# Two chunk pairs of the second output projection computed by seven block products, and the gate groups of the last decay head split into portions

## The reference

```python
# first block
x = x + y @ w_out            # pooling layer: y is 2048 wide, w_out 2048 x 1024
x = x + y @ w_out            # latent attention, 16 heads of 128: y 2048 wide
x = rmsnorm(x, final_norm)
# second block
h = rms_norm(x, g) @ w_in    # q, k, v, forget gates, z
attn = forgetting_attention(q, k, v, log_f)              # 8 heads of 64, with decay
sgu = zu * (w_s @ layer_norm(zv) + b_s)                  # 8 gate groups of 64
x = x + concat(rms_norm(attn), rms_norm(sgu)) @ w_out
x = x + (silu(gate) * up) @ w_down                       # 2816 wide
out = rms_norm(x, final_norm_g)
```

## Time and profile before

| | |
|---|---|
| median of 3 runs | 1300.34 us (1299.59 to 1300.74) |
| profiled execution | 1299.91 us, span 1298.2 us |
| granted clock of PE | 0.999 over the span |
| PE busy | 1289.8 us of the span, 99% |
| DVE, ACT, POOL busy | 871.9, 596.8, 461.3 us |

### The profile page before, as it was taken

The page is one execution under the profiler, slowest core; times in us unless marked ns, Lnnn a source line. Parts: engine busy times, 40 slices in busy tenths (PEclk is TensorE's granted clock), DMA queues, the critical chain, the costliest instruction groups (busy, mean ns, idle before and its releaser), DMA issues.

```text
span 1298.2 us, 17978 instructions
## 1 busy us (share of the span) xinstructions
PE 1289.8 (99%) x6934; PEld 1095.9 (84%) x6934; DVE 871.9 (67%) x1239; ACT 596.8 (46%) x989; POOL 461.3 (36%) x208
## 2 busy tenths in 40 slices
PE   9999999999999999999999999999999999999998
PEld 7888888898778888888888788898879999998886
DVE  7999726889292366665534574567989999985442
ACT  5223323435343465666733345568464444443223
POOL 2444544445444442443544343323430000015441
PEclk9999999999999999999999999999999999999999
DMA  4333423224722522325143345543323323323331
GB/s 164 98 98 106 123 88 97 77 85 139 274 84 89 145 55 77 82 68 210 49 162 98 115 147 147 132 114 114 98 66 130 98 99 118 111 83 113 114 96 67
DMA packets 47874, 143.64 MB, mean 111 GB/s; under 512 B 6032, under 2 KB 6032, under 8 KB 47024
## 3 DMA queue, kind: packets, MB, share of 16 engines
q1 hardware_dynamic: 43984, 129.88, 32.7%
q10 hardware_dynamic: 3808, 12.64, 2.8%
HBM read 121.46 MB, written 10.49 MB: 102 GB/s over the span
## 4 chain that ended last, share of the span: by engine, by line
PE 76%; issue 12%; POOL 6%; DVE 4%; ACT 2%; DMA 1%; POOLq 0%; SPq 0%; ACTq 0%
PE bank L2101 24%; PE bank L2103 23%; PE bank L2102 23%; POOL w_lo L700 6%; PE bank L2339 2%; PE bank L2328 1%; PE bank L2329 1%; DVE out_w L1400 0%; PE bank L2125 0%; DMA x<-x_in 0%; DVE out_t L1362 0%; DMA raw<-stream 0%; PE bank L2484 0%; PE bank L2485 0%; DVE y_lo L1366 0%
## 5 line engine op out<-in xcount | busy, mean ns | idle before, releaser
L700 POOL TENSOR_TENSOR w_lo<-raw,w_hi 128x1024 fp32r<-128x1024 f32 (+1 forms) x146 | 367.0, 2519 | 532.0 <-ACT w_hi L768 532.0
L768 ACT ACTIVATE w_hi<-raw 128x1024 fp32r<-128x1024 f32 x149 | 156.1, 1054 | 199.4 <-PE bank L2103 129.0
L745 POOL TENSOR_TENSOR w_lo<-raw,w_hi 128x1024 fp32r<-128x1024 f32 x22 | 53.6, 2439 | 263.0 <-DVE w_lo L1958 204.5
L2101 PE MATMUL bank<-pool_xg,w_hi 128*128 128x512 f32 x248 | 98.5, 397 | 0.2 <-POOL w_lo L700 0.2
L2102 PE MATMUL bank<-pool_xg,w_hi 128*128 128x512 f32 x248 | 98.1, 396 | 0.0
L2103 PE MATMUL bank<-pool_xg,w_lo 128*128 128x512 f32 x248 | 98.1, 395 | 0.0
L2101 PE MATMUL bank<-right,w_hi 128*128 128x256 f32 x336 | 94.4, 281 | 0.0
L2102 PE MATMUL bank<-right,w_hi 128*128 128x256 f32 x336 | 94.1, 280 | 0.0
L2103 PE MATMUL bank<-right,w_lo 128*128 128x256 f32 x336 | 94.1, 280 | 0.0
L2101 PE MATMUL bank<-y_hi,w_hi 128*128 128x512 f32 (+1 forms) x232 | 89.2, 385 | 0.0
L2102 PE MATMUL bank<-y_lo,w_hi 128*128 128x512 f32 (+1 forms) x232 | 89.0, 384 | 0.0
(11 more groups left out here) (451 smaller groups left out, 3628.2 us busy)
## 6 DMA issues: line engine op xcount, KB each, us to landing
raw<-stream SPq DMA_DIRECT2D x187, 512.0 KB, 3.7
raw_x<-stream SPq DMA_DIRECT2D x18, 512.0 KB, 4.8
spill<-x ACTq DMA_DIRECT2D x2, 2048.0 KB, 8.1
xg_spill<-mla_xg ACTq DMA_DIRECT2D x2, 2048.0 KB, 12.0
rope_q<-turned_hl SPq DMA_DIRECT2D x64, 64.0 KB, 2.6
zx<-xg_spill SPq DMA_DIRECT2D x2, 1536.0 KB, 9.8
stacked<-fq SPq DMA_DIRECT2D x24, 128.0 KB
stacked<-fk SPq DMA_DIRECT2D x24, 128.0 KB
```

Source lines behind the costliest of these rows:

```text
L700: pool.tensor_tensor(w_lo[:, j % RING, 0:width], raw[:, j % RAW, 0:width], plain(w_hi[:, j % RING, 0:width]), ALU.subtract).then_inc(tile_ ...
L745: pool.tensor_tensor(w_lo[:, s, 0:D], raw[:, d % RAW, 0:D], plain(w_hi[:, s, 0:D]), ALU.subtract).then_inc(tile_lo, 1)
L768: act.activation(w_hi[:, t % RING, 0:width], raw[:, t % RAW, 0:width], ACT.Copy).then_inc(tile_hi, 1)
L2101: pe.matmul(target, a_hi, b_hi, start=start, stop=False)
```

## The change

The four chunks 0 to 3 of the second projection get their second half by seven block products too, in two pairs. The first six `first` tiles come first, `first 0` still in head 15. Chunks 0 and 1 are added to `x` early, inside `right_operands`, since tile `("first", 5)` reuses the bank of chunk 1 and pair 0 that of chunk 0. `product_low` falls away, as `right_operands` makes those low parts. In the last decay head the gate groups are done in four portions of two, `square_sum(1)` goes ahead of the last head's output, and `split_mix(24)` goes ahead of ACT's wait for all 8 groups.

```diff
-             "mla_out": tuple((half, m) for m in range(DC) for half in ("first", "second"))}
-OUT_PAIRS = {"pool_out": 3}
+             "mla_out": (*(("first", m) for m in range(6)), ("direct", 0), ("crossed", 0), ("second", 4), ("direct", 1),
+                         ("crossed", 1), ("first", 6), ("second", 5), ("second", 6), ("first", 7), ("second", 7))}
+OUT_PAIRS = {"pool_out": 3, "mla_out": 2}
+TAKEN_BEFORE = {"pool_out": (1, 5, 6), "mla_out": (1, 4)}
+COMBINED_BEFORE = {"pool_out": ({}, {"s3": 2}, {"a11": 2, "s3": 4}), "mla_out": ({}, {"a12": 2})}
...
-                copies, casts = (5, 8, 11), (3, 6, 9)
-                squares = {7: (0, 1), 10: (2, 3)}
-                last_chunks = {13: (4, 5), 14: (6,)}
+                pooling = stage == "pool_out"
+                copies, casts = ((5, 8, 11), (3, 6, 9)) if pooling else ((6, 9), (4, 7))
+                squares = {7: (0, 1), 10: (2, 3)} if pooling else {8: (0, 1), 11: (2, 3)}
+                last_chunks = {13: (4, 5), 14: (6,)} if pooling else {12: (4,), 13: (5,), 14: (6,)}
...
             attn_square(FOX_PAIRS - 1)
+            split_mix(24)
             act.wait_ge(sgu_gated, SGU_G)
...
-            split_mix(24)
...
+                if stage == "mla_out":
+                    dve.wait_ge(x_back, 16)
+                    take(stage, 0)
+                    take(stage, 1)
                 t_block_low(1)
                 weight_sums(stage, 0)
...
-                if h == HEADS - 1:
-                    product_low(range(8, 14))
...
-            product_low(range(14, PC))
+            right_operands("mla_out", mla.out, 2 * PC)
...
-                    gate_groups(range(4))
+                    gate_groups(range(2))
                 transposed_low(fox, h, f_prob_t_hi, f_prob_t_lo, (2, 3))
...
-                    gate_groups(range(4, SGU_G))
+                    gate_groups(range(2, 4))
+                    settle(square_sum(1))
...
-            settle(square_sum(1))
             settle(square_sum(2))
+            gate_groups(range(4, 6))
             attn_low(FOX_PAIRS - 1)
             square_sum(3).then_inc(attn_summed, 1)
+            gate_groups(range(6, SGU_G))
             dve.wait_ge(attn_mean, 1)
```

More of the change, by code:

```diff
@@ L1039, in mix_square_chunk @@
                                scale=col("final_norm", k)).then_inc(n.squared, 1)
[L1041 to L1047, removed]
+            out_stage("mla_out", n, mix_gained_chunk, mix_square_chunk, first=1)
             act.dma_start(ln_g[:], rows_in[:, FOX_HEADS:FOX_HEADS + D_SGU]).then_inc(ln_in, 16)
@@ L1339, in norm_mean, with take @@
                 dve.reciprocal(mean_sq[:], mean_sq[:]).then_inc(n.prepared, 1)
+            def take(stage, m):
+                dve.wait_ge(tile_used, TILE[stage] + out_at(stage, "first", m) + 1)
+                dve.tensor_tensor(x[:, m, :], out_bank(stage, CHUNK_BANK[stage][m])[:], x[:, m, :], ALU.add).then_inc(bank_taken, 1)
             def right_operands(stage, ready, y_count):
@@ L1425, in total @@
                     sum_chunk(n, k, pairs)
-                for m in range(3):
-                    take(m)
+                for m in range(0 if stage == "pool_out" else 2, 3):
+                    take(stage, m)
                 weight_lows(0)
-                take(3)
-                take(4)
+                take(stage, 3)
+                if stage == "pool_out":
+                    take(stage, 4)
                 weight_sums(stage, 1)
@@ L1436, in residual @@
                 total(1)
[L1437 to L1451, removed]
+                if stage == "pool_out":
+                    take(stage, 5)
+                    weight_sums(stage, 2)
+                    combine(1)
+                    weight_lows(2)
+                    total(2)
+                    total(3)
+                    combine(2)
+                    dve.wait_ge(n.x_ready, 6)
+                    for k in range(6):
+                        low(k)
+                    take_last(6)
+                    total(4)
+                    total(5)
+                    low(6)
+                    total(6)
+                else:
+                    combine(1)
+                    dve.wait_ge(n.x_ready, 4)
+                    for k in range(4):
+                        low(k)
+                    total(2)
+                    total(3)
+                    for k in range(4, 7):
+                        take_last(k)
+                        low(k)
+                        total(k)
                 take_last(7)
@@ L1676, in _ @@
                 prepare_tile(0, j)
[L1677 to L1681, removed]
             peaks(mla, 0, MLA_SCALE, (0, 1, 2))
@@ L1705, in _ @@
                     dve.tensor_tensor(z[:, ZN + n, :], bank[6 + n % 2][:], inv[:], ALU.mult).then_inc(mla_evac, 1)
[L1708 removed]
+            right_operands("mla_out", mla.out, 2 * PC)
             n = norm["mix"]
[L1710 removed]
             pairs = [(mix_sqsum[:, i, :], lambda c, i=i: mix_sq[:, c % 2, i, :]) for i in range(2)]
[L1712 to L1717 removed]
+            residual("mla_out", n, mix_xg_hi, mix_xg_lo, lambda c: gain12[:, c:c + 1], pairs)
             dve.wait_ge(n.mean, n.before + 1)
@@ L1802, in gate_groups, with square_sum @@
                                              col("b_s", g), mine, ALU.add, ALU.mult).then_inc(sgu_gated, 1)
+            def square_sum(pair):
+                dve.wait_ge(attn_squared, pair + 1)
+                return dve.tensor_tensor(attn_sqsum[:], attn_sq[:, 0, :] if pair == 1 else attn_sqsum[:], attn_sq[:, pair, :], ALU.add)
             qk_evacuate(2)
@@ L2135, in out_tile @@
                         pe.wait_ge(y_lo_done, HALF_K * (stage == "mla_out") + k + 1)
-                    elif j == 1 and stage == "mla_out":
-                        pe.wait_ge(y_last_done, k - HALF_K + 1)
                     last = three(out_bank(stage, CHUNK_BANK[stage][m])[:], *wblock(t, i), y_hi[:, k, :], y_lo[:, k, :], k == 0,
@@ L2198, in out_product @@
                     elif kind != "crossed" and j >= first:
-                        if stage == "mla_out":
-                            out_tile(stage, j, range(8))
-                            continue
                         if (kind, i) == ("first", 5):
```

22 lines of the change are left out of this document (4 added, 18 removed).

## The result

The changed kernel took 1303.28 us (median of 22 runs, 1301.69 to 1305.32) beside 1300.62 us for the kernel before (22 runs, 1298.71 to 1303.09): a ratio of 1.0022, interval 1.0016 to 1.0028. It is slower by 2.7 us, or 0.22%. The prediction had put the edge between "the same" and "slower" at 0.2%, which lies inside this interval.

A forecast was written before the change was run, and what follows sets the result against it. PE was taken as the bound nearly everywhere. The projection's -2.44 + 0.9 = -1.5 us and the split's +4.0 gave +2.5 on 1299.91, 1302.4, and with 0.43 for the median 1302.8 us; range 1299.0 to 1305.0.

The forecast's parts named there:

- Matmuls: Second projection: seven products take 9.98 us a pair instead of 11.20 for two tiles, 2.44 us less for two pairs.
- The start costs nothing: Start of the second projection: PE's five first tiles cover DVE's chain with 27.2 us, so no wait before pair 0.
- The copy of pair 1: Second projection: PE waits at s2 for ACT's copy, behind a load and four squares; 0.9 us taken.
- The sum that meets POOL: End of head 7: the early square_sum(1) meets POOL's low, so PE's mean comes about 0.8 us later.
- The split: Behind the last decay head: ACT's early split of tile 24 waits for PE, delaying the squares; PE +4.0 us at transposes.
- The first rival: Nothing queued behind the early split matters, so only the projection's terms remain: 1297.4 to 1299.3 us; chance 0.15.
- The second: Rival: DVE and POOL meet neither at the projection's copy nor behind the last decay head: -0.5 us, 1299.8; chance 0.13.
- the third rival: DVE becomes the bound in the second projection, late for pair 0 or meeting POOL again: 1305 to 1306 us; chance 0.10.
- the fourth: Rival: the seven products save nothing, 84 small matmuls being held up by weight loads: 1305 us; chance 0.02.

The follow-up runs named there:

- e6: Changed kernel with the split of tile 24 back in its old place and square_sum(1) back behind the output copy: 1300.75 us, 1.0008 of before.
- e4: Kernel before with only the split of tile 24 moved ahead of the squares of zu: 1305.51 us, 1.0038 of before.
- e1: Changed kernel with the split of tile 24 put back behind the scaling of zu: 1302.59 us, 1.0011 of before.
- e9: As e6, but ACT holds the split of tile 24, and so POOL's lows, until DVE's first two attention additions are done: 1304.71 us, 1.0031 of before.
- e12: As e9, but ACT's split of tile 26 goes behind its four copies of the gated branch: 1299.34 us, 0.9986 of before.
- e5: As e2, with ACT's four squares of chunks 0 and 1 behind the copy of pair 1: 1297.62 us, 0.9979 of before.
- e2: Kernel before with only the second projection changed, last decay head and what follows as before: 1298.79 us, 0.9985 of before.
- e11: The kernel of e5 measured once more, beside e10: 1298.15 us, 0.9981 of before.
- e10: The kernel of e2 measured once more, beside e11: 1297.65 us, 0.9977 of before.
- e3: Kernel before with only the last decay head and what follows changed, projection as before: 1306.90 us, 1.0049 of before.
- e8: Changed kernel with 12 matmuls that serve nothing ahead of PE's wait at the transposes: 1301.48 us, 1.0008 of before.

## Why the prediction was right, point by point

The forecast was 1302.8 us, within 0.5 of the median: +2.5 us against +2.7 measured. The interval is clear of no change, but 0.22% lies on the edge of 0.2% that the prediction had set, so the measurement doesn't decide between its two large classes ("the same" 0.50, "slower" 0.44).

1. **Matmuls, 1.22 us a pair, 2.44 in all.** Shown: pair 0 took 9.97 us, forecast 9.98. In ten experiments' traces, where PE waits at no point of it, the stretch from `first 1` to the next norm's `mean` is 87.2 us, 2.5 less than before.
2. **The start costs nothing.** Shown: no wait of PE there in any trace. DVE's `z` ended at 650.75 in the changed kernel, forecast 650.3 from a start of PE that came 0.4 us later here.
3. **The copy of pair 1, +0.9.** This is the term that was mis-sized. The mechanism was there: from the split to the copy it is 4.2 us (697.51 - 693.32) where the first projection has 2.95, the 1.2 more that the squares were priced at. But the wait is 0.29 us in the changed kernel's trace and nothing in the ten others. DVE's weight sum met POOL, and the load's split came 3.7 us behind the sums (693.32 - 689.60), as for pair 2 of the first projection, not 5.3. Of the two rows for a load I took the slower, and the projection gained 2.2 here and 2.5 in the others, not 1.5.
4. **The sum that meets POOL, mean +0.8.** Shown: 1.97 us for the sum, the mean 0.7 later, and e6, without the early sum, has the mean where it was before.
5. **The split, PE +4.0 with the mean's 0.8 in it.** Shown: 0.7 + 3.3 = 4.0 us, one meeting with POOL. e4 shows that the split alone makes the 3.3. What the step didn't say is that groups 6 and 7 had taken a place on the same path: without the early split they make PE wait 2.4 us (e1, e6). "Queued behind the waiting split" was priced; "the other thing that the squares wait for" was not looked at.
6. **What was missing.** The half clock behind the wait, 2.6 us in the profiled execution and none in some others. Steps 1 to 5 as measured give +1.8; the median is 0.9 above that. The error of step 3 (0.7 too much) and this one (about 0.9 too little in the median) lie on opposite sides, so that the forecast came nearer than its parts. That much of it was luck.

The first rival is out by e4 and by ACT's 4.35 us of waiting: PE stood 3.21 us at the transposes for what was queued behind the split. The second failed at three places: 2.77, 1.97 and 2.12 us. e9 shows its mechanism from the other side: without POOL the additions take 0.69 each. In e1 the multiplication between them, with one operand in a bank, took 0.68 us beside the same low. The whole trace of the kernel before says the same. Of its rows of one 128x512 float32 TENSOR_TENSOR that overlap an instruction of POOL, the 37 with an operand in a bank took 0.68 to 0.69 us, while 12 of the 17 with both operands in SBUF took longer, up to 2.88. By the Trainium skill, GPSIMD Engine Reference, Key points, a DVE instruction with two SBUF inputs contends with GpSimd; the trace agrees. No row speaks for the third rival (PE had no wait before pair 0) or the fourth (9.97 us for a pair). The fourth, priced at 1305 us, had its 0.02 counted to "the same" where it belongs to "slower"; that changes nothing here.

## What to carry to other kernels

When an instruction that waits is moved ahead in an in-order queue, price everything behind it to the first engine that is the bound, then ask what else those instructions wait for: taking back one of two delays that lie side by side returns little (e1), and clearing one queue may show the next (e9, e12). A longer wait at a point doesn't say that the point comes later; take the distance to a common row ahead of it (e6). A wait of the bounding PE can cost more than its length, because the clock may be lower behind it. And a difference of 1 us between two kernels with 11 runs each should be measured twice before a cause is given to it (e5 and e2, then e11 and e10).

## What the hardware showed that I had not expected

PE waits of 3.2 us (changed kernel, e3, e4) and 5.0 us (e9) were followed in the traces by matmuls at a granted clock of 0.50, the 1.2 GHz level, costing 2.6 us in the changed kernel and 1.5 in e3 and e4; waits of 2.4 us (e1, e6) and 0.5 us (e8) were not. The length of the wait doesn't settle it, however. In e9 a wait of only 2.3 us in the first projection was followed by half clock as well. PE, and the window behind it:

```profile
300.26 0.36 PE L2104 MATMUL bank<-out_t,out_w 128*128 128x256 f32 x1 [2.27 <-ACT out_parts L860]
```

```profile
302.00:304.00 2.00, 2.00 (x11) 2.00 (x11) 1.96 (x2) 0.19 (x1) 1.08 (x1) 0.50 0.53 213
```

From 300.26 the next 24 matmuls took 4.4 us, where before they took 2.95: 1.5 us more. And e1 and e6 have runs with a lower mean clock than any of before beside them, though their traces show no fall. The cost isn't the same in each execution: some runs of the changed kernel had a mean clock of 1.000. Nor is the mean clock of a run exact to the last digit: one run of e1 is recorded with 0.949 and took 1301.59 us, no longer than its neighbours with 1.000.

A filled wait is thus not dearer than an idle one of the same length, and can be cheaper: e8 does 2.8 us more of matmuls, its transposes start no later (from the `mean` 15.57 us, against 15.51), and its median is 1.7 us below the changed kernel's, each against its own before.
